# Gated linear attention: scores in four row groups, and the second direction prepared within the first

## The chip, the cores and the metric

The kernel runs on one core of one Trainium2 chip. The metric is the device time of one execution in microseconds (us), lower is better.

## The reference

Two layers of a trunk over 256 context rows and 512 latent rows (768 in all, width 1024). Each layer has four parallel branches (latent attention, mLSTM, gated linear attention, differential attention), merged by sigmoid gates and one projection, and then a mixture of 16 experts. The change is in the gated linear attention (GLA), which runs in both directions, first over the context, then over the latents. For 4 heads, 32 key and 64 value columns each, in chunks of 64 rows:

```
gcum = cumsum(lg)                       # log decay within the chunk
g_end = gcum[-1]
s_loc = (k * exp(g_end - gcum))^T v     # what a chunk adds to the state
S_next = exp(g_end) * S + s_loc         # carried from chunk to chunk
q_dec = q * exp(gcum)
att = causal( q_dec (k * exp(-gcum))^T )
o = att v + q_dec S                     # summed over the two directions
```

In layer 0 outputs are needed for all six tiles of 128 rows, in the last layer for the four latent tiles alone; the states run over all rows in both.

## The kernel before

**Engines and order.** Each engine has its own program, written out by hand, and semaphores tie them. The tensor engine (PE) does the projections with `fm` and `tm`, then `gla(L)`. The scalar engine (ACT) evicts projections and takes the exponentials, the vector engine (DVE) does sums, masks and evictions of the rest. The order of the `wait_ge` and `then_inc` calls in the three `gla(L)` functions is the order in which things happen; an engine never passes a waiting instruction of its own.

**Merge units.** `merge_units(L, n)` on PE does n units of the branches' merge: 8 products with a gate weight and 2 with a branch weight, into one PSUM bank. `gates` on ACT takes its tanh, `merged` on DVE multiplies and adds and then frees the bank (`g_free`). Layer 0 has 24 such units within GLA, layer 1 has 16; they come from the branch before, and so are work that PE can do at any time in GLA. `gl_quota` says how many are done at which place. `stir` is a filler: products whose result nobody reads.

**Banks.** `ring(kind, banks)` gives a kind of result its PSUM banks, used in turn; `job(kind)` waits until the next is free. In GLA the units ("g") have five banks (6, 7, 0, 1, 2), all else ("d") has 3, 4 and 5.

**Directions.** `for d in range(2)` is done whole, one direction after the other. For each: DVE makes the cumulated decays (a scan, L1808) and their differences, ACT takes the exponentials (L1597 is behind that wait), and DVE multiplies keys and queries, and copies the queries into `g_qm`, which holds zeros for all heads but one in each of its four blocks. PE transposes the decayed keys (L534), DVE copies them (`g_ke`). Then 11 state products on PE (L898, 64 rows each); DVE takes each out of its bank with a head mask and adds it to the decayed state in the row of states `g_S` (two operations). Then come a filler of 8 products, a wait for all states, and the tiles: the scores of a tile are one product of 128 rows and 512 columns (L908), DVE masks them (`g_A`), and the output is two products with the state (L919, 64 columns of the array each) and four with the values (L922), which DVE copies or adds into `g_y`.

**The end.** Two units (`GL_END`), a filler of 6 products, and the transposes of `g_y` once DVE has normed it. In `finish` DVE signals `y_ready` and only then merges the two units. The differential branch follows with its projections (L527).

The functions that the diff touches:

Of the kernel before, what the change touches and what calls it, by code (L numbers as in the profile page):

```python
# [22 lines left out]
P = 128  # L23
# [135 lines left out]
def hybrid_layers(nc, I, out, stop=None):  # L159
    ctx = ExitStack()  # L160
    with ctx:
# [31 lines left out]
        def pk(name):  # L193
# [13 lines left out]
                 "rows_in", "rows_t", "xs", "gu", "silu", "hid", "hid_t", "hid_f", "ys", "ys_a", "ys_d", "scat", "put", "sel_t", "sel_c", "fsum", "fsum_free", "df_ready"] + [f"f_back{t}" for t in range(NT)]  # L207
# [93 lines left out]
        def gl_quota(L):  # L301

            q = [(6, 2, (1, 0, 1, 0, 1, 1)), (4, 2, (1, 0, 1, 0, 1, 1))] if len(chunks(L)) == 3 else \
                [(5, 1, (1, 0, 1, 0)), (3, 1, (1, 0, 1, 0))]
            assert sum(a + b + sum(x) for a, b, x in q) + GL_END == branch_units(L)
            return q

# [74 lines left out]
        g_t1, g_t2 = area(4 * T, T), area(5 * T, T)  # L382
        g_a = area(6 * T, 2 * T).rearrange("p (d t) -> p d t", d=2)
        g_qd = area(6 * T, T)
        g_ki = area(7 * T, T)
        g_qm = area(8 * T, 4 * T).rearrange("p (h t) -> p h t", h=4)
        g_ke = area(12 * T, T)
        g_v = area(13 * T, NT * 256).rearrange("p (t c) -> p t c", t=NT)
        g_S = area(15 * T, 12 * 256).rearrange("p (c n) -> p c n", c=12)
        g_y = area(19 * T, NT * 256).rearrange("p (t c) -> p t c", t=NT)  # L390
        g_A = (area(21 * T, 512), g_t1[:, 0:512])
        g_sl = area(21 * T + 512, 256)
        g_sc = area(15 * T, NT * 256)

# [85 lines left out]
        def _(pe):  # L480
# [380 lines left out]
            def gla(L):  # L861
# [16 lines left out]
                quota = gl_quota(L)  # L878
# [6 lines left out]
                ring("g", (6, 7, 0, 1, 2))  # L885
                for d in range(2):

                    at_start, at_states, at_step = quota[d]
                    merge_units(L, at_start)
# [3 lines left out]
                    pe.wait_ge(sems["d_free"], st["d"])  # L893
                    for i in range(11):
# [3 lines left out]
                        pe.matmul(b[:, 0:256], g_ke[r:r + 64, t * P:(t + 1) * P], g_v[r:r + 64, t, :],  # L898
                                       start=True, stop=True).then_inc(sems["d_done"], 1)
                        if i == 5:  # L900
                            merge_units(L, at_states // 2)
# [4 lines left out]
                    def scores(t):  # L906
                        b = job("d")
                        pe.matmul(b[:, :].rearrange("p (h c) -> p h c", h=4), g_ki[:, t * P:(t + 1) * P],  # L908
                                       g_qm[:, :, t * P:(t + 1) * P], start=True, stop=True).then_inc(sems["d_done"], 1)

                    scores(QT[0])
                    for i, t in enumerate(QT):
                        if i + 1 < len(QT):
                            scores(QT[i + 1])
                        merge_units(L, at_step[i])
                        pe.wait_ge(sems["gl_att"], c.nth("gl_att"))
                        b = job("d")
                        for r in range(2):
                            pe.matmul(b[r * 64:r * 64 + 64, 0:256], g_qd[:, t * P + r * 64:t * P + r * 64 + 64],  # L919
                                      g_S[:, 2 * t + r, :], start=True, stop=False, skip_group_check=True)  # L920
                        for h in range(4):
                            ins = pe.matmul(b[:, h * 64:h * 64 + 64], g_A[i % 2][:, h * P:(h + 1) * P],  # L922
                                            g_v[:, t, h * 64:h * 64 + 64], start=False, stop=True, skip_group_check=True)
                        ins.then_inc(sems["d_done"], 1)
# [368 lines left out]
        def _(act):  # L1293
# [257 lines left out]
            def gla(L):  # L1551
# [29 lines left out]
                act.sem_inc(sems["gl_in"], 1)  # L1581
                for d in range(2):

                    do((g_t1, g_t2)[d], g_lg[:, d, :], AF.Abs)
                    do((g_t1, g_t2)[d], (g_t1, g_t2)[d], AF.Exp, scale=-1.0)
                    do((g_t1, g_t2)[d], (g_t1, g_t2)[d], AF.Ln, bias=ones[:, 0:1])
                act.sem_inc(sems["gl_l"], 1)
                quota = gl_quota(L)
                for d in range(2):
                    gates(L, 2 * (d == 0))  # L1590
                    act.wait_ge(sems["gl_g"], c.nth("gl_g"))

                    do(g_t1, g_t1, AF.Exp)
                    do(g_t2, g_lg[:, d, :], AF.Exp, scale=-1.0)
                    do(g_lg[:, d, :], g_lg[:, d, :], AF.Exp)
                    do(s_ge[:, d, :], s_ge[:, d, :], AF.Exp)
                    act.sem_inc(sems["gl_e"], 1)  # L1597
                    at_start, at_states, at_step = quota[d]
                    gates(L, at_start - 2 * (d == 0) + at_states + sum(at_step))
# [184 lines left out]
        def _(dve):  # L1784
# [387 lines left out]
            def gla(L):  # L2172
                quota = gl_quota(L)
                S(dve.memset(g_qm, 0.0))
                dve.wait_ge(sems["gl_in"], c.nth("gl_in"))
                dve.wait_ge(sems["gl_l"], c.nth("gl_l"))
                for d in range(2):
                    x = g_lg[:, d, :]
                    ts(x, x, 0.0, ALU.min)
                    tt(x, x, (g_t1, g_t2)[d], ALU.subtract)  # L2180
                    ts(x, x, 1.0 / 16, ALU.mult)
                merged(L, 2)
                for d in range(2):
                    x = g_lg[:, d, :]

                    xs_ = x if d == 0 else x[:, ::-1]
                    o_ = g_t2 if d == 0 else g_t2[:, ::-1]
                    scan(o_, cc("resets"), xs_, 0.0, ALU.mult, ALU.add)
                    copy(x, g_t2)
                    xc = x.rearrange("p (c l) -> p c l", l=64)  # L2190
                    end = xc[:, :, 63] if d == 0 else xc[:, :, 0]
                    copy(s_ge[:, d, :], end)
                    t1 = g_t1.rearrange("p (c l) -> p c l", l=64)
                    tt(t1, s_ge[:, d, :].unsqueeze(2).to_broadcast([P, 12, 64]), xc, ALU.subtract)
                    dve.sem_inc(sems["gl_g"], 1)
                    at_start, at_states, at_step = quota[d]
                    dve.wait_ge(sems["gl_e"], c.nth("gl_e"))
                    q0 = QS[-1][0]
                    tt(g_t1, g_t1, g_k, ALU.mult)
                    tt(g_ki, g_t2, g_k, ALU.mult)  # L2200
# [654 lines left out]
```

## Time and profile before

| | us |
|---|---|
| median of three runs | 3803.69 (3802.13 to 3811.6) |
| profiled execution, its own time | 3800.9 |
| its span | 3799.2 |
| PE busy | 3474.8 (91%) |
| DVE busy | 1117.7 (29%) |
| ACT busy | 716.6 (19%) |
| GLA of layer 0, from its first merge unit to the next branch | 581.7 to 764.5 |
| GLA of layer 1, likewise | 2548.3 to 2689.2 |

The span is what the profile sees; the execution's own time is 1.7 us more. Times of rows are counted from the span's start. A float32 product of two operands appears as two records on PE, a transpose as one. The granted clock of PE is 1.0 at 2.4 GHz and 0.5 at 1.2 GHz.

### The profile page before, as it was taken

To read this page: it belongs to the slowest core of one execution; us is meant where nothing else is said; L and a number is where in the kernel's file an instruction comes from. 1 tells how busy PE (TensorE), PEld (TensorE's weight loads), DVE (VectorE), ACT (ScalarE), POOL (GpSimd) and SP (SyncE) were. 2 spreads that over 40 slices of the span, in tenths; PEclk is the share of its full clock that TensorE was granted. 3 is DMA by queue.
4 is the path that set the end of the run, shared out by engine and by line. 5 is a ranking of instruction groups with operands and counts; after the bars stand their busy time and mean duration, and the time that the engine had idled before them with its cause. 6 is when DMAs were issued, how large, how long until landed. Compare 5 with 4: busy or idle time off the path is not lost.

```text
span 3799.2 us, 66279 instructions
## 1 busy us (share of the span) xinstructions
PE 3474.8 (91%) x27942; PEld 2414.8 (64%) x27942; DVE 1117.7 (29%) x2486; ACT 716.6 (19%) x1366; POOL 130.4 (3%) x188
## 2 busy tenths in 40 slices
PE   7899999999999999999999999998999998888887
PEld 4456756768875677766777666756677664444443
DVE  1433324425533411111111443315165231111112
ACT  2313212112223100000000422221132210010101
POOL 0000100000000000000000000000000000000000
PEclk9999999999999999999999999898999999999999
DMA  5511010020022999999999302020111259999998
GB/s 214 228 39 48 23 56 23 13 77 29 28 100 89 363 360 370 371 348 356 360 367 349 135 1 75 23 78 12 62 44 49 89 237 408 408 410 414 411 411 328
DMA packets 102941, 741.32 MB, mean 195 GB/s; under 512 B 8224, under 2 KB 14496, under 8 KB 60720
## 3 DMA queue, kind: packets, MB, share of 16 engines
q1 hardware_dynamic: 90512, 692.67, 46.3%
q0 software_dynamic: 12192, 45.14, 4.1%
q8 instruction: 191, 3.13, 0.3%
q14 instruction: 46, 0.38, 0.0%
HBM read 712.57 MB, written 25.21 MB: 194 GB/s over the span
## 4 chain that ended last, share of the span: by engine, by line
PE 67%; DMA 20%; DVE 6%; ACT 3%; issue 2%; SPq 0%; DVEq 0%; POOL 0%; ACTq 0%; POOLq 0%
PE psum L625 13%; PE psum L1127 10%; PE psum L527 7%; DMA ring<-in_w_e_down 7%; PE psum L520 5%; PE psum L1157 5%; DMA ring<-in_w_e_gate 4%; PE psum L983 4%; DMA work<-in_w_e_gate 3%; PE psum L627 3%; DMA ring<-in_w_e_up 3%; PE psum L1118 3%; DMA ring<-in_w_ada 2%; PE psum L852 2%; DVE work L1793 2%
## 5 line engine op out<-in xcount | busy, mean ns | idle before, releaser
L625 PE MATMUL psum<-HT,ring 128*128 128x256 f32 x2560 | 615.1, 396 | 19.3 <-DVEq L1871 8.5
L625 PEld LDWEIGHTS psum<-HT,ring 128*128 128x128 f32 x2560 | 502.0, 199 | 120.0 <-issue 29.6
L1127 PE MATMUL psum<-work,ring 128*64 128x96 f32 x11264 | 486.2, 247 | 49.3 <-issue 35.0
L1127 PEld LDWEIGHTS psum<-work,ring 128*64 128x64 f32 x11264 | 471.3, 137 | 66.1 <-issue 52.1
L1118 PE MATMUL psum<-ring,work 128*64 128x256 f32 x1024 | 253.1, 405 | 66.6 <-DMA ring<-in_w_e_gate 52.2
L1298 ACT ACTIVATE work<-psum,small 128x768 f32<-128x768 f32 (+3 forms) x208 | 146.0, 702 | 712.1 <-PE psum L1163 321.1
L527 PE MATMUL psum<-ring,HT 128*128 128x512 f32 (+1 forms) x768 | 276.0, 521 | 0.0
L1118 PEld LDWEIGHTS psum<-ring,work 128*64 128x64 f32 x1024 | 144.4, 145 | 162.9 <-DMA ring<-in_w_e_gate 62.8
L1119 PE MATMUL psum<-ring,work 128*64 128x256 f32 (+1 forms) x1024 | 244.0, 384 | 0.0
L1301 ACT ACTIVATE work<-psum 128x256 f32<-128x256 f32 (+8 forms) x227 | 107.4, 473 | 657.3 <-PE psum L527 236.9
L1157 PE MATMUL psum<-ring,work 128*64 128x512 f32 x960 | 220.1, 598 | 9.3 <-DMA ring<-in_w_e_down 9.3
L527 PEld LDWEIGHTS psum<-ring,HT 128*128 128x128 f32 x768 | 145.8, 190 | 127.3 <-issue 120.5
L520 PE MATMUL psum<-HT,ring 128*128 128x256 f32 (+5 forms) x688 | 216.1, 475 | 0.3 <-issue 0.3
L1797 DVE TENSOR_SCALAR work<-psum,small 128x64 f32<-128x64 f32 (+2 forms) x154 | 68.6, 445 | 457.6 <-PE psum L1163 204.4
L1298 ACT ACTIVATE X<-psum 128x384 f32<-128x384 f32 (+3 forms) x112 | 43.4, 387 | 732.9 <-PE psum L1127 411.0
L520 PEld LDWEIGHTS psum<-HT,ring 128*128 128x128 f32 (+2 forms) x688 | 123.2, 181 | 90.4 <-issue 76.0
L1298 ACT ACTIVATE YT<-psum,pack 128x256 f32<-128x256 f32 x160 | 75.9, 474 | 554.0 <-PE psum L627 503.6
L627 PE MATMUL psum<-YT 128*128 128x256 f32 x640 | 164.2, 379 | 0.0
L1793 DVE TENSOR_TENSOR work<-X,psum 128x384 f32<-128x384 f32 (+1 forms) x48 | 25.0, 521 | 416.8 <-PE psum L1127 416.8
L1157 PEld LDWEIGHTS psum<-ring,work 128*64 128x64 f32 x960 | 67.7, 136 | 123.0 <-issue 111.5
L983 PE MATMUL psum<-ring,X 128*128 128x512 f32 x320 | 140.5, 598 | 4.1 <-DVEq L2285 2.1
L1793 DVE TENSOR_TENSOR X<-X,psum 128x256 f32<-128x256 f32 (+1 forms) x64 | 22.5, 352 | 408.8 <-PE psum L1119 408.2
(208 smaller groups left out, 3981.3 us busy)
## 6 DMA issues: line engine op xcount, KB each, us to landing
ring<-in_w_e_gate SPq DMA_DIRECT2D x64, 2048.0 KB, 12.0
ring<-in_w_e_up SPq DMA_DIRECT2D x48, 2048.0 KB, 13.2
ring<-in_w_e_down SPq DMA_DIRECT2D x48, 2048.0 KB, 10.3
ring<-in_w_ada SPq DMA_DIRECT2D x24, 2048.0 KB, 9.9
ring<-in_w_e_up SPq DMA_DIRECT2D x32, 1536.0 KB, 10.8
ring<-in_w_gate SPq DMA_DIRECT2D x16, 2048.0 KB, 8.7
HT<-in_w_e_up SPq DMA_DIRECT2D x16, 2048.0 KB, 24.8
ring<-in_w_e_gate SPq DMA_DIRECT2D x16, 1536.0 KB
```

Source lines behind the costliest of these rows:

```text
L520: ins = pe.matmul(b[0:M, 0:n], w[:, k, c0:c0 + M], HT[:, k, off:off + n], start=(k == 0), stop=(k == KD - 1))
L527: ins = pe.matmul(b[:, 0:n], HT[:, k, t * P:(t + 1) * P], w[:, k, c0:c0 + n], start=(k == 0), stop=(k == KD - 1))
L625: pe.matmul(b[:, 0:256], w[:, k, d4 * P:(d4 + 1) * P], HT[:, k, off:off + 256], start=(k == 0), stop=(k == KD - 1))
L627: ins = pe.matmul(b[:, 256:512], wbr[:, m % 2, i, d4 * P:(d4 + 1) * P], YT[:, n_ % 2, i, off:off + 256], start=(i == 0), stop=(i == 1))
L983: ins = pe.matmul(b[:, :], mT[:, k, t * P:(t + 1) * P], w[:, k, :], start=(k == 0), stop=(k == KD - 1))
L1118: pe.matmul(b[0:64, 0:256], e_xs[:, k, 0:64], w[:, k, 0:256], start=(k == 0), stop=(k == KD - 1))
L1119: ins = pe.matmul(b[64:128, 0:n - 256], e_xs[:, k, 0:64], w[:, k, 256:n], start=(k == 0), stop=(k == KD - 1))
L1127: ins = pe.matmul(b[lo:lo + 64, f * cap:(f + 1) * cap], w[:, k, c0:c0 + 64], e_xs[:, k, 0:cap], start=(k == 0), stop=(k == KD - 1))
L1157: ins = pe.matmul(banks[6 + half][lo:lo + CAP_L, :], e_hidT[:, at, 0:CAP_L], w[:, k % 2 if split else k, half * 512:half * 512 + 512], sta ...
L1298: c.seq(act.activation(*a, **kw))
L1301: c.seq(act.activation(dst, src, AF.Copy))
L1793: S(dve.tensor_tensor(o_, a, b, op))
```

## The change

Scores: `g_qm` goes. Each tile's scores are now four products of 32 rows and 128 columns, one for each head, with keys and decayed queries as they lie in the partitions, each head into a bank of its own (0 to 3). Two tiles are done at a time, side by side in the four banks.

Order: the fillers of 8 products go. The first direction's 11 states are made in pieces of 4, 4 and 3 with a unit behind each, through four banks. The second direction's sums, exponentials, operands, transposed keys and states are made between the first direction's tiles, as `gl_ahead` says: for each tile whether keys are turned behind it, and which states come ahead of and behind its units. The states get a second row (`g_S[d]`). From the first scores on the units have two banks (6, 7) and all else has two (4, 5).

DVE's scaling by 1/16 moves into ACT's exponentials, and two of its operations become one. ACT takes the two logarithms' parts side by side and signals each.

```diff
+            q = (4, 3, ((2, 2, 1, 1, 1, 1), (2, 1, 1, 1, 1, 1))) if len(chunks(L)) == 3 else (4, 3, ((1, 1, 1, 1), (1, 1, 1, 0)))
...
+        def gl_ahead(L):
+            if len(qtiles(L)) == 6:
+                return (0, 0, 0, 0), (0, 0, 0, 0), (1, 0, 0, 0), (0, 0, 2, 4), (0, 4, 6, 8), (0, 8, 10, 11)
+            return (0, 0, 0, 0), (1, 0, 0, 0), (0, 0, 3, 6), (0, 6, 9, 11)
...
-                ring("g", (6, 7, 0, 1, 2))
-                for d in range(2):
...
-                    merge_units(L, at_states - at_states // 2)
-                    stir("g", 8)
...
+                ring("d", (2, 3, 4, 5))
+                ring("g", (6, 7, 0, 1))
+                merge_units(L, at_start)
+                opened = st["g"]
+                pe.wait_ge(sems["g_free"], opened - 2)
+                rings["g"].append((opened, (6, 7)))
...
+                def states(d, first, last):
+                    if last and not first:
+                        pe.wait_ge(sems["d_free"], st["d"])
+                    for i in range(first, last):
...
+                def scores(d, first):
+                    for i in range(first, first + 2):
+                        t = QT[i]
+                        at = (i % 2) * P
+                        for h in range(4):
+                            r = slice(32 * h, 32 * h + 32)
+                            ins = pe.matmul(g_scores[:, h, at:at + P], g_ki[d][r, t * P:(t + 1) * P], g_lg[r, d, t * P:(t + 1) * P],
+                                            start=True, stop=True)
+                    ins.then_inc(sems["gl_sc"], 1)
...
+                turn_keys()
+                for x in range(at_states):
+                    states(0, 4 * x, min(4 * x + 4, 11))
+                    merge_units(L, 1)
+                pe.wait_ge(sems["gl_ops"], c.nth("gl_ops"))
+                pe.wait_ge(sems["g_free"], opened)
+                ring("d", (4, 5))
+                scores(0, 0)
+                for d in range(2):
...
+                    for i in range(len(QT)):
+                        turn, a, b, z = gl_ahead(L)[i] if d == 0 else (0, 0, 0, 0)
+                        states(1, a, b)
+                        merge_units(L, at_step[d][i])
+                        states(1, b, z)
+                        if i % 2 == 0 and i + 2 < len(QT):
+                            pe.wait_ge(sems["gl_att"], gl_masked(L, d, i + 1))
+                            scores(d, i + 2)
+                        step(d, i)
+                        if turn:
+                            turn_keys()
```

ACT:

```diff
+                def decays(d):
+                    act.wait_ge(sems["gl_g"], c.nth("gl_g"))
+                    do(g_t1, g_t1, AF.Exp, scale=1.0 / 16)
                     act.sem_inc(sems["gl_e"], 1)
+                    do(g_lg[:, d, :], g_ki[d], AF.Exp, scale=1.0 / 16)
+                    do(g_ki[d], g_ki[d], AF.Exp, scale=-1.0 / 16)
+                    do(s_ge[:, d, :], s_ge[:, d, :], AF.Exp, scale=1.0 / 16)
+                    act.sem_inc(sems["gl_e"], 1)
...
+                gates(L, 2)
+                decays(0)
+                gates(L, at_start - 2 + at_states + at_step[0][0])
+                decays(1)
+                gates(L, sum(at_step[0][1:]) + sum(at_step[1]))
```

DVE, the tiles (`sums`, `keys` and `operands` are the parts of what was done ahead of each direction, `turned_keys` the copies of the transposed keys):

```diff
                     for i, t in enumerate(QT):
+                        turn, a, b, z = gl_ahead(L)[i] if d == 0 else (0, 0, 0, 0)
+                        states(1, a, b)
+                        merged(L, at_step[d][i])
+                        states(1, b, z)
                         dve.wait_ge(sems["d_done"], c.nth("d_done"))
...
+                        if i + 2 < len(QT):
+                            masked(d, i + 2)
+                        if d == 0:
+                            if i == 0:
+                                sums(1)
+                            if i == 1:
+                                keys()
+                                operands(1)
+                            if turn:
+                                turned_keys()
```

## Rows read from the trace of the kernel before

**Rows 1.** The page, the chain that ended last, by engine
```profile
PE 67%; DMA 20%; DVE 6%; ACT 3%; issue 2%; SPq 0%; DVEq 0%; POOL 0%; ACTq 0%; POOLq 0%
```
**Rows 2.** Windows of all engines: stretch, length, busy us (records) each, clock, DMA, GB/s
```profile
core 0: us, PE busy (x) PEld busy (x) DVE busy (x) ACT busy (x) POOL busy (x), PEclk, DMA share, GB/s
581.70:764.50 182.80, 168.89 (x761) 130.37 (x762) 86.96 (x163) 31.30 (x46) 0.00 (x0) 0.93 0.06 21
2548.30:2689.20 140.90, 129.69 (x540) 97.71 (x541) 70.71 (x136) 27.51 (x38) 0.00 (x0) 0.87 0.06 19
612.20:625.80 13.60, 9.86 (x23) 6.20 (x24) 9.60 (x23) 0.95 (x2) 0.00 (x0) 0.50 0.00 0
```
**Rows 3.** Timeline of PE, layer 0, first units and the first direction's states
```profile
start us, us, engine line op out<-in xcount [idle before <-releaser]
581.71 5.27 PE L625 MATMUL psum<-HT,ring 128*128 128x256 f32 x16 [1.09 <-ACTq L1580]
...
587.68 3.62 PE L625 MATMUL psum<-HT,ring 128*128 128x256 f32 x16
...
592.00 3.62 PE L625 MATMUL psum<-HT,ring 128*128 128x256 f32 x16
...
610.88 0.87 PE L534 MATMUL psum<-const,work 128*128 128x128 f32 x6 [1.45 <-DVEq L2204]
612.95 2.07 PE L898 MATMUL psum<-work 64*128 64x256 f32 x6 [1.19 <-DVEq L2209]
618.02 3.42 PE L898 MATMUL psum<-work 64*128 64x256 f32 x6 [2.99 <-DVEq L2219]
...
628.07 1.13 PE L898 MATMUL psum<-work 64*128 64x256 f32 x6
```
**Rows 4.** Timeline of PE, layer 0, filler, scores and output steps
```profile
635.56 3.62 PE L504 MATMUL psum<-const 128*128 128x256 f32 x16
639.01 1.88 PE L908 MATMUL psum<-work 128*128 128x512 f32 x4
640.73 3.62 PE L625 MATMUL psum<-HT,ring 128*128 128x256 f32 x16
...
645.14 0.65 PE L919 MATMUL psum<-work 128*64 128x256 f32 x4
...
646.66 1.08 PE L908 MATMUL psum<-work 128*128 128x512 f32 x2
```
**Rows 5.** Timeline of PE, differential branch, scores of 32 rows (two row groups)
```profile
854.71 0.70 PE L747 MATMUL psum<-work 32*128 32x256 f32 x4
855.34 0.33 PE L534 MATMUL psum<-const,work 128*128 128x128 f32 x1
```
**Rows 6.** Timeline of DVE, layer 0, the last row from layer 1
```profile
592.51 0.56 DVE L1797 TENSOR_SCALAR work<-work 128x768 f32<-128x768 f32 x1 [83.01 <-ACTq L1587]
...
598.92 1.76 DVE L1808 TENSOR_TENSOR_SCAN work<-const,work 128x768 f32<-128x768 f32 x1
...
618.58 0.42 DVE L1793 TENSOR_TENSOR work<-psum,const 128x256 f32<-128x256 f32 x1
...
619.68 0.42 DVE L1793 TENSOR_TENSOR work<-psum,const 128x256 f32<-128x256 f32 x1
...
640.14 0.69 DVE L1793 TENSOR_TENSOR work<-psum,const 128x512 f32<-128x512 f32 x1 [2.85 <-PE psum L908]
...
645.80 0.42 DVE L1805 SCALAR_TENSOR_TENSOR YT<-YT,psum 128x256 f32<-128x256 f32 x1 [4.03 <-ACTq L1351]
...
761.29 0.42 DVE L1805 SCALAR_TENSOR_TENSOR YT<-YT,psum 128x256 f32<-128x256 f32 x1
...
2687.29 0.42 DVE L1805 SCALAR_TENSOR_TENSOR YT<-YT,psum 128x256 f32<-128x256 f32 x1
```
**Rows 7.** Timeline of ACT, layer 0, the exponentials of one direction
```profile
602.56 2.59 ACT L1298 ACTIVATE work<-work 128x768 f32<-128x768 f32 x3 [7.66 <-DVEq L2195]
```
**Rows 8.** Timeline of PE, units after the last step (749.55, 2677.05), layer 1's second
```profile
749.55 3.67 PE L625 MATMUL psum<-HT,ring 128*128 128x256 f32 x16
...
2555.70 3.62 PE L625 MATMUL psum<-HT,ring 128*128 128x256 f32 x16
...
2677.05 3.67 PE L625 MATMUL psum<-HT,ring 128*128 128x256 f32 x16
```

More of the change, by code:

```diff
@@ L911, in gla @@
[L911 to L924, printed above, removed]
+                                  start=True, stop=True).then_inc(sems["d_done"], 1)
@@ new lines, in step @@
+                def step(d, i):
+                    t = QT[i]
+                    pe.wait_ge(sems["gl_att"], gl_masked(L, d, i))
+                    b = job("d")
+                    for r in range(2):
+                        pe.matmul(b[r * 64:r * 64 + 64, 0:256], g_lg[:, d, t * P + r * 64:t * P + r * 64 + 64],
+                                  g_S[d][:, 2 * t + r, :], start=True, stop=False, skip_group_check=True)
+                    for h in range(4):
+                        ins = pe.matmul(b[:, h * 64:h * 64 + 64], g_A[i % 2][:, h * P:(h + 1) * P],
+                                        g_v[:, t, h * 64:h * 64 + 64], start=False, stop=True, skip_group_check=True)
+                    ins.then_inc(sems["d_done"], 1)
@@ L2172, in gla @@
             def gla(L):
[L2173 to L2177, printed above, removed]
-                    x = g_lg[:, d, :]
[L2179 to L2194, printed above, removed]
+                at_start, at_states, at_step = gl_quota(L)
@@ L2195, in gla, with keys @@
                     dve.sem_inc(sems["gl_g"], 1)
[L2196 removed]
+                def keys():
                     dve.wait_ge(sems["gl_e"], c.nth("gl_e"))
[L2198 removed]
                     tt(g_t1, g_t1, g_k, ALU.mult)
[L2200 to L2203 removed]
@@ L2209, in gla, with states @@
                         dve.sem_inc(sems["d_free"], 1)
-                    merged(L, at_start - 2 * (d == 0))
-                    heads = cc("heads").unsqueeze(2).to_broadcast([P, 4, 64])
-                    S(dve.memset(g_S[:, gla_chunk(d, 0), :], 0.0))
-                    for i in range(11):
+                def states(d, first, last):
+                    if last and not first:
+                        S(dve.memset(g_S[d][:, gla_chunk(d, 0), :], 0.0))
+                    for i in range(first, last):
                         a, z = gla_chunk(d, i), gla_chunk(d, i + 1)
@@ L2234, in gla, with masked @@
-                    masked(0)
+                        stt(g_S[d][:, z, :], g_S[d][:, a, :], s_ge[:, d, a:a + 1], g_sl, ALU.mult, ALU.add)
+                    if last == 11 and first < last:
+                        dve.sem_inc(sems["gl_state"], 1)
+                def masked(d, i):
+                    mask = cc(("m_fwd", "m_bwd")[d]).unsqueeze(1).to_broadcast([P, 4, P])
+                    at = (i % 2) * P
+                    if i % 2 == 0:
+                        dve.wait_ge(sems["gl_sc"], c.nth("gl_sc"))
+                    tt(g_A[i % 2].rearrange("p (h c) -> p h c", h=4), g_scores[:, :, at:at + P], mask, ALU.mult)
+                    dve.sem_inc(sems["gl_att"], 1)
@@ new lines, in gla @@
+                dve.wait_ge(sems["gl_in"], c.nth("gl_in"))
+                sums(0)
+                merged(L, 2)
+                keys()
+                operands(0)
+                merged(L, 1)
+                turned_keys()
+                merged(L, at_start - 3)
+                for x in range(at_states):
+                    states(0, 4 * x, min(4 * x + 4, 11))
+                    if x:
+                        merged(L, 1)
+                masked(0, 0)
+                masked(0, 1)
+                merged(L, 1)
```

97 lines of the change are left out of this document (44 added, 53 removed).

## The prediction

> **What bounds the kernel now.** The page comes first: the chain that ended last runs 67% through the tensor engine and 20% through DMA [rows 1], and its DMA parts are weights of the experts and of the modulation, not of this branch. The change touches two stretches, the gated linear attention of layer 0 (182.8 us) and of layer 1 (140.9 us) [rows 2]. In both the tensor engine (PE) is the engine to follow: the projections before it and the differential branch after it start when PE gets to them, so what a stretch loses or gains moves the end one for one. The timeline shows where PE doesn't do dense work there: it waits for the first operands (1.45 us), for the copied keys (1.19) and for VectorE (DVE), which evicts the states (2.99) [rows 3]. Around these waits the granted clock is half (0.50, which is 1.2 GHz) for 13.6 us [rows 2]; of PE's 9.9 busy us there about half, 4.9, is the clock's price. Then come 16 filler records, 635.56 to 639.01, 3.45 us, and the scores of two tiles take 1.72 us [rows 4].
>
> **Prices.** A merge unit (20 records) is 4.32 us of PE (587.68 to 592.00); the first one of a stretch is slow, 5.97 us in layer 0, 7.4 in layer 1 [rows 3, 8]. One output step (both halves of the carried state, four heads) is 1.52 us, 645.14 to 646.66 [rows 4]. Six records (three state products) take 1.13 us, part of it latency [rows 3]: I take 0.25 us a product. DVE: a state costs 1.10 us (618.58 to 619.68), the scan 1.76, masking a tile 0.69, an operation on 256 columns 0.42, so a merge of two 1.0 with its gaps; it begins about 0.75 us after PE's last product of the unit, for ScalarE's tanh lies between [rows 4, 6]. ScalarE (ACT) needs for three exponentials 2.59 us [rows 7].
>
> **What is removed.** (1) Two fillers of 3.45 us a layer: 13.8 us in all. (2) The states' lumps. Before, PE sits behind the state chain of 11 x 1.1 us in both directions, with at most one or two units as cover. Now the first direction's eleven are cut by three units, the second's lie between units of the first's steps. Waits of 1.45, 1.19 and 2.99 us and the half clock behind them go, but see the new waits. DVE's early work (scaling, a copy, the masked queries) goes as well. It waits till 592.51 for both directions' logarithms [rows 6]; with one it starts some 3 us earlier, at 589 by my estimate, and sums (4.0), exponential, two merges (2.1) and a multiplication (1.0) make the first keys by 597, while PE asks for them at 600.6. The first wait is gone, and DVE's removed operations themselves count for nothing, since PE's units cover them (uncovered they would be 7 us a direction). (3) The scores. Per tile there were 512 columns in one product; now four products of 32 rows and 128 columns, each in its own bank.
>
> **Price of the scores.** No row shows four groups at once. Two groups of 32 rows do stand there: four records of 256 columns from 854.71 to 855.34, 0.63 us [rows 5], where four such records of full height take 0.86 (a fifth of a unit's 20 records). So groups overlap; 0.43 us is what one group streams, 0.2 is load and drain. Two tiles on four groups stream 0.43 us as well: with the same 0.2 and some issue time I take 0.75 a pair of tiles. The bounds are 0.65 and, without overlap, today's 1.72. Ten pairs (6 in layer 0, 4 in layer 1) save 9.7 us by it, 0 at the other bound. The Trainium skill (TensorEngine Tiling (Array Packing), Theoretical Speedup) allows up to 4x for 32 rows; that would be 0.43 a pair, 3 us more gained and a time of 3755. The same page (Key Properties) says that a change of tiling mode drains the engine, which speaks against cutting products small: each pair now has two such changes. The trace agrees: ahead of the step's 64-column tiles a unit takes 4.41 us instead of 4.32 [rows 3, 4], 0.1 us, which is inside my 0.2.
>
> **The new waits, layer 0.** From 581.7: 22 units up to the last step (5.97 + 21 x 4.32 = 96.7), 6 score pairs 4.5, 12 steps 18.2, 22 states 5.5, keys turned twice 1.4: 126.3 us of PE. Waits: the first keys' copies 1.35 (as 612.95 shows). Where the second direction's keys are turned, behind step 2 of the first, PE needs the bank of that step's output, and DVE copies the output, masks a tile (0.69) and then the keys (1.26): 2.2 us. The ring for states and outputs has now two banks. In tiles 3 and 4 two states follow a unit at once, and the output step then needs the bank of the first of them, which DVE reads only behind tanh and merge: 0.75 + 1.0 + 0.45 after the unit's end, less 0.45 of PE's own work: 1.8 us, twice; twice 0.5 for the state that waits for the output's copy; 0.4 for the last state. Together 8.6 us. The last step ends at 581.7 + 134.9 = 716.6, before at 749.55 [rows 8]: 33.0 us earlier. For the clock behind these waits of 1.8 to 2.2 us I charge 2.5 us (a half-clock spell costs 1.65 us as at 581.71 to 4.9 as at 612.2; some of them will meet one).
>
> **Layer 1.** 14 units 7.4 + 13 x 4.32 = 63.6, scores 3.0, 8 steps 12.2, states 5.5, keys 1.4: 85.7 us. Here the keys are to be turned after step 1 already, and only one unit and one step (5.8 us) lie between step 0 and that. What must happen behind step 0 is a chain over two queues: output copied 0.7, tile masked 0.85, DVE's sums for direction 1 (subtraction 0.96, scan 1.76, ends 0.2, difference 0.96: 4.0), ACT's exponentials 2.9. Behind these in ACT's queue stands the tanh of unit 9 (0.6), behind that in DVE's queue its merge 1.1, the copy 0.45, masking 0.75, and then the keys' multiplication 1.0, with 0.3 of handovers: 12.6 us. **PE stands 6.8 us**, then 2.3 more while DVE finishes queries and copies keys. The tiles 2 and 3 take three states each after and before their unit on two banks: 2.6, 0.9 and 1.85 us by the reckoning above, and 1.35 at the start: 15.8 us of waits, and 4.5 for the clock (one full spell, a part of another). The last step ends at 2548.3 + 106.0 = 2654.3, before at 2677.05, where the unit behind it starts [rows 8]: 22.7 us earlier, the clock counted.
>
> **The tail.** The filler at the end (12 records of 0.216 us, 2.6) stays, but the merge units now go through two banks where there were five. It must therefore wait for the merge of the last unit but one, and that stands in DVE's queue behind the whole head norm: at 761.29, 11.7 us after the last step, in layer 1 at 2687.29, 10.2 us after it [rows 6, 8]. Two units cover 8.7 us of that. In layer 0 PE idles 3.6 us, then fills 2.6, then turns the outputs over two banks: 17.2 us from the last step to the next branch where there were 14.9. In layer 1 14.3 where there were 12.2. With a clock spell behind 3.6 us of idling (3.4 us, between the 1.65 and 4.9 above) and a third of one in layer 1: 5.7 and 3.1 us given back.
>
> **Sum.** Layer 0: 33.0 - 2.5 - 5.7 = 24.8. Layer 1: 22.7 - 3.1 = 19.6. Together 44.4 us. The profiled execution took 3800.9 us (span 3799.2), 2.8 below the median of 3803.7: 3756.5 by the one, 3759.3 by the other; I take 3758. Nothing later should eat it: what DMA has in the chain lies elsewhere [rows 1], and loads are issued when a buffer is freed, so they move along with PE.
>
> **Rivals.** *The row groups don't overlap* (that part of the change does nothing). For it: no row shows more than two at once. Against: those two do [rows 5]. 9.7 us less: 3768.
> *The clock falls behind each new wait.* There are eight places of 1.8 us or more; at 4.9 us each that is 39 us, where I charged 11.4: 3786. For it: 1.45 and 1.19 us close together were enough at 612.2 [rows 2, 3]. Against: most new waits stand alone between dense units.
> *Slower than before:* the first direction's steps run at half clock throughout, since a wait returns every 6 us there. Its 11 units in layer 0 and 7 in layer 1 would cost 4.32 us more each, 78, of which 7 are charged: 3829. It decides from 13 of these 18 units on. Against: with waits up to 3 us in their lumps, the stretches of before still keep a mean clock of 0.93 and 0.87 [rows 2].
> *The gain is given back* in the expert stages, where DMA has its 20% of the chain: 3800. For it: they don't get shorter. Against: they begin with loads asked for only when this branch and the next are through.
>
> **How the numbers follow.** Forecast 0.67, no overlap 0.12, clock at each wait 0.13, given back 0.05, slower 0.03. The likeliest's own range is 3745 to 3772: at one end the clock holds (11 us less) and scores take 0.65 (1 less), at the other its price is half as high again (6) and layer 1's queues lag by some 8 us more. The range 3744 to 3778 takes in the first rival and leaves out the last two, most of the second and a little of the first, some 0.2. A measurement of this kernel can tell about 0.3% (11 us) from no change. Faster by more: 0.67 + 0.12 + 0.13 = 0.92; within: 0.05; slower: 0.03.
>
> **What would show it.** In the changed profile: no 16-record filler in the stretches; score groups of 32 rows, 16 records within 0.75 us (1.7 would be the first rival); in layer 1 an idle time of about 6.8 us before keys are transposed, released by DVE, and none such in layer 0; idle times near 1.8 us before steps that follow states; before the last filler 3.6 us in layer 0 and 2.0 in layer 1, released by DVE's merge; stretches of about 158 and 121 us. The prediction is wrong if the stall in layer 1 is absent (9 to 12 us more gained), if a stretch's granted clock falls below 0.85, or if the time between and behind the stretches changes.

## The result, and the profile after

The changed kernel takes **3778.07 us** (median of 6, 3772.09 to 3788.13), the kernel before 3806.78 on the same chip (6, 3802.13 to 3811.6): ratio **0.993, 95% interval 0.9915 to 0.9945**. It is faster, by 28.7 us, where 3758 was forecast (a gain of 45.7 from 3803.69). The range ended at 3778, and 3778.07 lies just above it.

The page's chain that ended last reads nearly as before [rows 1]:

```profile
PE 69%; DMA 21%; DVE 5%; ACT 2%; issue 2%; SPq 0%; DVEq 0%; POOL 0%; ACTq 0%; POOLq 0%
```

The two stretches, from the first unit to the differential branch, and a part of layer 0, as windows; they answer to [rows 2]:

```profile
580.40:748.50 168.10, 157.22 (x801) 125.16 (x801) 79.69 (x150) 28.76 (x44) 0.00 (x0) 0.91 0.08 28
2535.90:2665.60 129.70, 113.66 (x556) 89.09 (x557) 64.27 (x123) 24.96 (x36) 0.00 (x0) 0.87 0.10 32
650.90:681.60 30.70, 27.17 (x96) 19.52 (x97) 12.63 (x29) 0.95 (x2) 0.00 (x0) 0.72 0.00 1
```

They are 14.7 and 11.2 us shorter than before, 25.9 together. The granted clock is no better: 0.91 and 0.87, where it was 0.93 and 0.87. In the third row it is 0.72.

PE's timeline of the changed kernel, layer 0: first unit, states and scores (answering to [rows 3, 4]), the steps that carry the second direction's states, and the tail [rows 8]; then layer 1.

```profile
580.41 6.47 PE L633 MATMUL psum<-HT,ring 128*128 128x256 f32 x16 [1.09 <-ACTq L1620]
...
587.59 3.62 PE L633 MATMUL psum<-HT,ring 128*128 128x256 f32 x16
...
596.22 3.62 PE L633 MATMUL psum<-HT,ring 128*128 128x256 f32 x16
...
600.54 0.82 PE L542 MATMUL psum<-const,work 128*128 128x128 f32 x6
602.63 1.13 PE L914 MATMUL psum<-work 64*128 64x256 f32 x8 [1.27 <-DVEq L2254]
...
608.20 1.14 PE L914 MATMUL psum<-work 64*128 64x256 f32 x8
609.27 3.72 PE L633 MATMUL psum<-HT,ring 128*128 128x256 f32 x16
...
613.78 1.13 PE L914 MATMUL psum<-work 64*128 64x256 f32 x6
...
619.35 0.73 PE L924 MATMUL psum<-work 32*128 32x128 f32 x16
620.01 3.72 PE L633 MATMUL psum<-HT,ring 128*128 128x256 f32 x16
...
651.03 1.23 PE L914 MATMUL psum<-work 64*128 64x256 f32 x4 [1.81 <-DVEq L2254]
652.19 4.74 PE L633 MATMUL psum<-HT,ring 128*128 128x256 f32 x16
...
660.13 0.65 PE L934 MATMUL psum<-work 128*64 128x256 f32 x4 [1.70 <-DVEq L2265]
...
664.13 5.58 PE L633 MATMUL psum<-HT,ring 128*128 128x256 f32 x16
...
672.91 0.65 PE L934 MATMUL psum<-work 128*64 128x256 f32 x4 [1.70 <-DVEq L2265]
...
676.39 6.27 PE L633 MATMUL psum<-HT,ring 128*128 128x256 f32 x16
...
728.02 3.67 PE L633 MATMUL psum<-HT,ring 128*128 128x256 f32 x16
...
740.30 5.49 PE L512 MATMUL psum<-const 128*128 128x256 f32 x12 [3.42 <-DVEq L1918]
...
2595.25 1.54 PE L542 MATMUL psum<-const,work 128*128 128x128 f32 x6 [6.74 <-DVEq L2239]
2598.49 1.23 PE L914 MATMUL psum<-work 64*128 64x256 f32 x4 [1.70 <-DVEq L2254]
2600.36 1.22 PE L914 MATMUL psum<-work 64*128 64x256 f32 x2 [0.64 <-DVEq L2265]
2601.51 6.28 PE L633 MATMUL psum<-HT,ring 128*128 128x256 f32 x16
...
2649.60 3.67 PE L633 MATMUL psum<-HT,ring 128*128 128x256 f32 x16
...
2660.37 4.54 PE L512 MATMUL psum<-const 128*128 128x256 f32 x12 [1.92 <-DVEq L1918]
```

The reader is to see three things. The waits stand where they were forecast and nearly as long: 1.27, 1.81, twice 1.70, 6.74, then 3.42 and 1.92 ahead of the last filler. Two tiles' scores take 0.66 us (619.35 to 620.01), so the four row groups do overlap. And the 16 records of a unit, 3.62 us at full clock, take 4.74, 5.58 and 6.27 behind waits of 1.7 to 1.8 us, and 6.28 in layer 1: that is the clock, whose mean over this part is 0.72 (third window).

### The profile page after: what moved, and what is told of

Its sections match the earlier page's. It is cut to its first block, busy times and chain, and to the rows that moved or that the text cites. A ratio compares the mean times of both kernels' runs of the same rounds, so it can differ in the third digit from the quotient of the medians.

```text
span 3778.2 us, 66347 instructions
## 1 busy us (share of the span) xinstructions
PE 3457.1 (92%) x27998; PEld 2409.6 (64%) x27998; DVE 1099.1 (29%) x2456; ACT 711.7 (19%) x1362; POOL 130.8 (3%) x188
## 4 chain that ended last, share of the span: by engine, by line
PE 69%; DMA 21%; DVE 5%; ACT 2%; issue 2%; SPq 0%; DVEq 0%; POOL 0%; ACTq 0%; POOLq 0%
PE psum L633 14%; PE psum L1167 8%; PE psum L535 7%; DMA ring<-in_w_e_down 7%; PE psum L1197 6%; PE psum L528 5%; DMA ring<-in_w_e_gate 5%; DMA ring<-in_w_e_up 4%; PE psum L1023 4%; PE psum L635 3%; PE psum L1158 3%; PE psum L755 2%; DMA work<-in_w_e_gate 2%; PE psum L1203 2%; PE psum L773 2%
## 5 line engine op out<-in xcount | busy, mean ns | idle before, releaser
L1197 PEld LDWEIGHTS psum<-ring,work 128*64 128x64 f32 x960 | 68.8, 137 | 123.8 <-issue 113.7
## 6 DMA issues: line engine op xcount, KB each, us to landing
HT<-in_w_e_up SPq DMA_DIRECT2D x16, 2048.0 KB, 24.8
```

The source lines that it names most:

```text
L1197: ins = pe.matmul(banks[6 + half][lo:lo + CAP_L, :], e_hidT[:, at, 0:CAP_L], w[:, k % 2 if split else k, half * 512:half * 512 + 512], sta ...
```

## The experiments

Each kernel was run beside the kernel before, both on the same chip; the ratio is to that kernel, and kernels of different chips are compared by it. The table takes the two stretches of each profile together, from windows like those above. **Idle** is length less PE's busy time. **Clock** is (1 - granted clock) x length for each stretch, added: what the lower clock costs if PE is busy throughout, so an upper bound, and good to some 1.5 us, since the clock is given to 0.01.

| kernel | ratio (95%) | stretches | sum | idle | clock |
|---|---|---|---|---|---|
| before | 1 | 182.8, 140.9 | 323.7 | 25.1 | 31.1 |
| b_nofill | 0.9956 (0.9938-0.9975) | 175.1, 134.5 | 309.6 | 26.1 | 31.1 |
| changed | 0.993 (0.9915-0.9945) | 168.1, 129.7 | 297.8 | 26.9 | 32.0 |
| a_again | 0.9933 (0.9912-0.9953) | 168.2, 129.3 | 297.5 | 26.9 | 31.9 |
| e_serial | 0.995 (0.9934-0.9967) | 165.5, 127.7 | 293.2 | 26.9 | 26.9 |
| e_fill | 0.9882 (0.9854-0.991) | 157.8, 119.8 | 277.6 | 3.0 | 5.6 |
| e_beside | 0.9979 (0.9965-0.9992) | 166.2, 135.1 | 301.3 | 26.5 | 11.4 |
| e_thin32 | 0.9928 (0.99-0.9956) | 161.5, 130.3 | 291.8 | 1.9 | 20.8 |
| e_thin64 | 0.9893 (0.9863-0.9923) | 157.8, 118.5 | 276.3 | 2.7 | 4.4 |
| e_sums_early | 0.9917 (0.9891-0.9943) | 166.2, 119.2 | 285.4 | 21.5 | 21.1 |
| e_states_first | 0.9898 (0.9874-0.9921) | 164.9, 122.0 | 286.9 | 25.5 | 21.3 |
| e_tail | 0.9923 (0.9892-0.9953) | 159.9, 125.9 | 285.8 | 22.7 | 23.1 |
| e_best1 | 0.9889 (0.9873-0.9906) | 160.3, 113.6 | 273.9 | 15.3 | 16.0 |
| e_best2 | 0.9917 (0.99-0.9933) | 160.3, 112.6 | 272.9 | 9.8 | 14.8 |
| e_fill_sums | 0.987 (0.9851-0.9888) | 158.9, 113.2 | 272.1 | 3.3 | 6.6 |
| e_best3 | 0.985 (0.983-0.987) | 156.5, 108.6 | 265.1 | 4.0 | 4.2 |

**The changed kernel again** (a_again, unaltered).

> The changed kernel unaltered, as the measure for the two beside it. 3778 us, ratio to before 0.993; stretches about 168 and 130 us with half-clock spells behind the new waits.

The stretches repeat within 0.4 us. The rest doesn't repeat: between the stretches this execution took 1774.4 us (743.0 to 2517.4) where the first took 1787.4 (748.5 to 2535.9), in one and the same code. So the stretches are read to a microsecond from one profile, and the total only from its interval. Even a stretch can move: e_serial's layer 0, with the same 10.9 us of waits, is 2.6 us shorter at a clock of 0.93.

**Fillers in the new waits** (e_fill): if the waits take the clock, products whose result nobody reads give it back.

```diff
                 turn_keys()
+                stir("g", 3)
...
+                        if b and not a:
+                            stir("g", 4)
                         states(1, a, b)
                         merge_units(L, at_step[d][i])
                         states(1, b, z)
+                        if d == 0 and z - b == 2:
+                            stir("g", 4)
...
                         if turn:
+                            if L == 1:
+                                stir("g", 15)
                             turn_keys()
                 merge_units(L, GL_END)
+                stir_bank(banks[0], 8 if L == 0 else 4)
                 stir("g", 6)
```

Four more stand before layer 1's third state of tile 2.

> The changed kernel with filler products put into its new waits on PE, about as long as each wait (1.3 us for the first copied keys, 1.7 before each output step behind states and for the second copied keys, 6.5 in layer 1 before the keys are turned, 3.5 and 1.7 before the last filler); the waits themselves stay. If the half clock behind the waits is what the forecast had too small, the slow units, products and fillers behind them (11 us in each layer by the profile after) come back: some 22 us less than the changed kernel, about 3756 us, and a mean clock of 0.98 or more in both stretches. If the slow stretches have another cause (products of 64 rows, transposes), the time stays within 5 us of the changed kernel's 3778.

Windows of e_fill, both stretches, and layer 0 around the states:

```profile
576.30:734.10 157.80, 156.71 (x847) 126.01 (x848) 79.72 (x150) 28.75 (x44) 0.00 (x0) 0.98 0.09 29
2515.20:2635.00 119.80, 117.86 (x625) 94.27 (x626) 64.33 (x123) 24.95 (x36) 0.00 (x0) 0.98 0.09 30
643.50:674.00 30.50, 30.17 (x151) 21.93 (x150) 16.22 (x36) 1.42 (x3) 0.00 (x0) 1.00 0.10 32
```

And the filler in layer 1's long wait, from its timeline:

```profile
2567.32 6.69 PE L512 MATMUL psum<-const 128*128 128x256 f32 x30
```

The clock is 1.00 where it was 0.72. 57 products of 0.432 us, 24.6 us, took the place of 23.9 us of idle time (26.9 less 3.0), and still the stretches are 20.2 us shorter: 20.2 + 24.6 - 23.9 = **20.9 us is the clock's price** behind the new waits, by this balance.

**Is it the idle time, or what stands around it?** The same 57 fillers, behind the waits instead of in them (e_beside), and the fillers in the waits but over 32 or 64 rows (e_thin32, e_thin64). In e_beside they stand behind the states, the output step or the old filler that waited. The 15 of the long wait come later: behind it are first the turned keys, a further wait and three states, then these fillers, from 2606.75 on.

```diff
                         states(1, a, b)
+                        if b and not a:
+                            stir("g", 4 if L == 0 else 19)
                         merge_units(L, at_step[d][i])
...
                         step(d, i)
+                        if d == 0 and z - b == 2:
+                            stir("g", 4)
```

> The same 57 filler products as in the run with fillers in the waits, but each put behind the instruction that waited, so that the waits stay. They are 24.6 us of products (57 x 0.432). If the waits themselves lower the clock, nothing is won back: idle time 27 and clock cost about 29 us as in the changed kernel, stretches about 178 and 144 us, time 3803, ratio to before 1.000. If it was the thin work around the waits (products of 32 and 64 rows) and full products close by repair it, the clock cost falls to the 5.5 us of the first units: stretches about 167 and 134 us, time 3781, ratio 0.994.

PE's timeline of e_beside, layer 0 and the long wait of layer 1, and its two windows:

```profile
654.85 0.70 PE L914 MATMUL psum<-work 64*128 64x256 f32 x4 [1.81 <-DVEq L2263]
655.48 2.00 PE L512 MATMUL psum<-const 128*128 128x256 f32 x8
657.32 3.62 PE L633 MATMUL psum<-HT,ring 128*128 128x256 f32 x16
...
664.13 0.65 PE L936 MATMUL psum<-work 128*64 128x256 f32 x4 [1.70 <-DVEq L2274]
...
2600.49 1.54 PE L542 MATMUL psum<-const,work 128*128 128x128 f32 x6 [6.73 <-DVEq L2248]
...
2606.75 9.68 PE L512 MATMUL psum<-const 128*128 128x256 f32 x38
```
```profile
582.90:749.10 166.20, 155.31 (x847) 125.76 (x848) 79.65 (x150) 28.73 (x44) 0.00 (x0) 0.98 0.08 29
2541.30:2676.40 135.10, 119.53 (x625) 95.64 (x626) 64.24 (x123) 24.93 (x36) 0.00 (x0) 0.94 0.09 31
```

The waits are all there (26.5 us idle), and in layer 0 none lowers the clock, not the one of 3.4 us at the tail either. In layer 1 it still falls at the wait of 6.73 us (the six records behind it take 1.54 us, 0.82 at full clock). So my theory, that each wait takes the clock, falls: with full products close behind, the waits of 1.6 to 1.8 us cost themselves alone in this profile. The stretches are as the second theory had them, 166 and 135 for 167 and 134. The time, 3789.93, is 9 us above its forecast, and the ratio 0.005 (19 us) above the changed kernel's, of which the stretches explain 3.5 us; the rest lies outside them and isn't explained.

```diff
+                    pe.matmul(b[:, 0:256], ident[0:32, :], const[0:32, 0:256], start=True, stop=True)
```

> The fillers stand in the waits as in the run that filled them, same number and same 256 columns each, but every product is over 32 rows of the array instead of 128 (only the 6 products of the old filler at the end keep 128). PE is then busy in the waits all the same. If idle time is what takes the clock, it holds as with full fillers: granted clock 0.98 in both stretches, 158 and 120 us, ratio to before 0.988. If rows count, so that thin products are as good as none, the clock falls where it fell in the changed kernel: granted clock about 0.91 and 0.87, stretches about 168 and 130 us, ratio 0.993.

> The same with fillers over 64 rows, the height of the state products. If idle time takes the clock: 0.98, stretches 158 and 120 us, ratio 0.988. If rows count: between that and the changed kernel, granted clock about 0.95 and 0.92, stretches about 163 and 125 us, ratio 0.990.

PE's timeline of e_thin32, the tail of layer 0, then layer 1:

```profile
735.48 4.26 PE L516 MATMUL psum<-const 32*128 32x256 f32 x16
739.67 5.49 PE L512 MATMUL psum<-const 128*128 128x256 f32 x12
...
2587.47 8.81 PE L516 MATMUL psum<-const 32*128 32x256 f32 x30
2596.22 1.54 PE L552 MATMUL psum<-const,work 128*128 128x128 f32 x6
```

PE is not idle there (0.9 us in the whole stretch of layer 1), and the clock falls all the same: 30 records take 8.81 us where the 30 of full height in e_fill take 6.69, and layer 1's mean is 0.89. The 64-row ones hold it as the full ones do (0.98, 0.99). In layer 0's middle even the 32-row ones, 8 records at a time, hold it; only its tail falls, where 16 of them take 4.19 us (735.48 to 739.67), and the 12 full-height records behind them 5.49. What these runs show is that the clock fell behind idle time and behind long busy time of 32 rows alike, and that short waits with dense work close behind did not bring it down. The Trainium skill (TensorE: Matmul & The Clock Gate, HAM oscillation) explains the loss by idle gaps; e_thin32 shows a loss without a gap.

**The waits one by one.** Layer 1's long wait: the second direction's sums before the first masks, and its keys behind tile 0 instead of 1 (e_sums_early). DVE takes the states ahead of the merge (e_states_first). No wait before the last filler (e_tail).

```diff
+                sums(1)
                 masked(0, 0)
                 masked(0, 1)
...
                             if i == 0:
-                                sums(1)
-                            if i == 1:
                                 keys()
                                 operands(1)
```
```diff
                         states(1, a, b)
-                        merged(L, at_step[d][i])
                         states(1, b, z)
+                        merged(L, at_step[d][i])
```
```diff
                 merge_units(L, GL_END)
-                stir("g", 6)
+                stir_bank(banks[0], 6)
+                ring("d", (3, 4, 5))
```

In the first, ACT's exponentials move ahead of the steps' gates too.

> The changed kernel, with the second direction's sums on DVE ahead of the first masks and its exponentials on ACT ahead of the unit's tanh that follows, and its keys and queries one tile earlier. If layer 1's wait of 6.74 us is the chain of sums, exponentials, tanh and merge, 1 to 3 us of it are left and the spell behind it is shorter: 5 to 9 us less, 3769 to 3773 us. If DVE's queue as a whole is the limit there, the wait only moves to the first scores and the time stays.

> The changed kernel, only DVE takes the states behind a unit before it merges that unit. If the output step waits for a bank because the merge stands ahead of the state in DVE's queue, the waits of 1.70 us (two in layer 0) and 1.60, 0.49 and 1.69 (layer 1) shrink to 0.7 or less, 5 to 6 us, and with them go the half-clock spells of layer 0's last two tiles and part of layer 1's: 10 to 17 us less than the changed kernel, 3761 to 3768 us. If the two banks themselves are too few, whatever the order, the waits stay and so does the time (3778).

> The changed kernel with the last filler in bank 0, which is free, so that it doesn't wait for the merge of the last unit but one, and three banks for the transposes behind it. If that wait (3.42 and 1.92 us) and the half clock behind it are the tail's loss, the time from the last step to the next branch goes from 20.5 to 15 us in layer 0 and from 16.0 to 12.2 in layer 1: 9 us less, 3769 us. If the tail is bound by the head norm (signalled 11.6 us after the last step) it gains 5 us or less.

PE's timeline of e_sums_early, layer 1; then of e_states_first, layer 0:

```profile
2588.24 1.10 PE L937 MATMUL psum<-work 128*128 128x64 f32 x8
2589.18 0.61 PE L542 MATMUL psum<-const,work 128*128 128x128 f32 x4
```
```profile
665.51 0.65 PE L934 MATMUL psum<-work 128*64 128x256 f32 x4 [0.73 <-DVEq L2265]
...
668.63 0.70 PE L914 MATMUL psum<-work 64*128 64x256 f32 x2 [0.80 <-DVEq L2309]
669.25 3.72 PE L633 MATMUL psum<-HT,ring 128*128 128x256 f32 x16
...
678.32 1.22 PE L914 MATMUL psum<-work 64*128 64x256 f32 x2 [0.80 <-DVEq L2309]
679.47 6.24 PE L633 MATMUL psum<-HT,ring 128*128 128x256 f32 x16
```

The 6.74 us are gone, as their cause, DVE's and ACT's queues, would have it; layer 1 is 10.5 us shorter. In e_states_first each 1.70 became 0.73 or 0.74 and a new 0.80: the sum of idle time is hardly smaller (25.5), yet the stretches are 3.2 and 7.7 us shorter, for the clock's bound went from 32.0 to 21.3. The first such pair of waits left the clock up (the unit behind it takes 3.72), the second brought it down (6.24).

One wait and its neighbours don't settle it, then. The wait of 1.81 us ahead of the second direction's first states, with the same products around it, was followed by a slow unit in the changed kernel (4.74) and by one at full clock in e_sums_early, whose layer 0 differs only in DVE's and ACT's order:

```profile
652.71 0.70 PE L914 MATMUL psum<-work 64*128 64x256 f32 x4 [1.81 <-DVEq L2254]
653.35 3.72 PE L633 MATMUL psum<-HT,ring 128*128 128x256 f32 x16
```

So the single spells can't be booked to single waits; the sums over a stretch can be compared. e_tail takes 8.2 and 3.8 us from the stretches, the idle time and the slow filler; by its total alone it can't be told from the changed kernel.

**The parts of the gain.** The four heads' scores issued head by head (e_serial), and the kernel before without its four fillers (b_nofill: `stir("g", 8)` left out).

```diff
-                    for i in range(first, first + 2):
...
-                        for h in range(4):
+                    for h in range(4):
+                        for i in range(first, first + 2):
```

> The changed kernel with the score products of a pair of tiles issued head by head, so that neighbours in the queue share a row group and can't overlap. If the overlap of the four groups is what makes a pair take 0.66 us, it goes to 1.5 to 1.8 us, and ten pairs cost 8 to 11 us more than in the changed kernel: 3787. If order doesn't matter to the overlap, the pair stays at 0.7 and the time at 3778.

> The kernel before without its four fillers of 16 records (3.45 us each), nothing else. If they cover no wait and keep no clock, all of it is gained: 13.8 us less than before. If they hide the end of the state chain or hold up the clock, 5 us or less.

```profile
618.81 0.75 PE L924 MATMUL psum<-work 32*128 32x128 f32 x16
619.49 3.72 PE L633 MATMUL psum<-HT,ring 128*128 128x256 f32 x16
```

Head by head the 16 records of e_serial take 0.68 us (above), tile by tile they took 0.66. So the order of issue within the group is of next to no account. b_nofill gains 7.7 and 6.4 us of its stretches, 14.1 where 13.8 were booked, and costs no clock (31.1 before and after): half of what the change takes off its stretches is to be had by this alone.

**Together.** e_best1 is the three edits of the waits. e_best2 adds 3 and 4 fillers where the keys are copied, e_best3 also 2 in each wait of 0.7 us or more among the states. e_fill_sums is e_fill with the early sums and without the 15.

> The changed kernel with three edits at once: states ahead of the merge on DVE, the second direction's sums early, the last filler in a free bank. Their stretches alone were 3.2, 1.9 and 8.2 us shorter in layer 0 and 7.8, 10.5 and 3.8 in layer 1 than the changed kernel's 168.1 and 129.7. If each takes away its own wait and the spell behind it, they add up: 155 and 110 us (the edits of layer 1 share some spells), 30 to 35 us less than the changed kernel, some 3745. If they only shift one limit of DVE's queue, the sum is nearer to the best single one: 3765.

> As the one with three edits, and fillers of 1.3 us while the first keys are copied and of 1.7 us while the second direction's are. If the two spells left come from these waits, a clock of 1.0 from there on, 2 to 5 us less than without the fillers; if the waits alone are too short to lower the clock, no change.

> The fillers in the waits (all but the one of 15 products in layer 1), and the second direction's sums and keys made earlier, so that the 6.8 us wait of layer 1 which that filler covered is gone. If clock and wait are two separate costs, both gains add: stretches 158 and about 111 us, 28 us less than the changed kernel, 3748, ratio to before 0.986. If the filler in the long wait was hiding the same cost as the early sums remove, it stays at the 0.988 of the fillers alone.

> States ahead of the merge, early sums, no wait at the tail, and fillers of 2 to 4 products in every wait of 0.7 us or more that was left. If even waits of 0.73 and 0.80 us cost the clock, it is now 1.0 throughout both stretches: 152 and 108 us, about 3745, ratio to before 0.985. If those short waits did not lower the clock, no gain over the same kernel without fillers (3757, ratio 0.989).

PE's timeline of e_best2, and windows of e_best3 behind the slow first unit:

```profile
653.67 0.65 PE L934 MATMUL psum<-work 128*64 128x256 f32 x4 [0.73 <-DVEq L2269]
...
656.78 1.22 PE L914 MATMUL psum<-work 64*128 64x256 f32 x2 [0.80 <-DVEq L2314]
657.93 6.23 PE L633 MATMUL psum<-HT,ring 128*128 128x256 f32 x16
```
```profile
587.00:737.70 150.70, 147.77 (x818) 118.12 (x817) 79.12 (x149) 23.10 (x39) 0.00 (x0) 1.00 0.06 19
2530.00:2631.20 101.20, 100.11 (x557) 79.19 (x556) 63.75 (x122) 17.87 (x29) 0.00 (x0) 1.00 0.06 17
```

e_best1 fell between its two forecasts: its three edits had taken 35.3 us from the stretches one by one, together they take 23.9, so they share spells or waits. In e_best2 two waits of 0.73 and 0.80 us among 64-row states still bring half the clock. Its time came out 7 us above e_best1's, with stretches 1.0 us shorter. With 0.9 us of products in each of them (e_best3) the clock is 1.00 to the end, the stretches 7.8 us shorter, the time **3743.87 us (3740.15 to 3755.93), ratio 0.985**: the best kernel, 29 us ahead of the changed one beside it (3772.91); its layer 0 is 4.5 us longer than forecast. e_fill_sums had stretches of 158.9 and 113.2 us for 158 and 111: wait and clock are two costs, and both gains add, but for some 3 us.

## Why the prediction was right, and where wrong

**Right by mechanism.** PE sets the stretches. The long wait of layer 1 measured 6.74 us for 6.8; the waits that follow states 1.70 for 1.8, and the tail's 3.42 and 1.92 for 3.6 and 2.0, in the places named. Up to the last step the waits sum to 6.7 us (8.6) and 14.1 (15.8). The first keys' wait was taken as 1.35, though its row has 1.19 [rows 3]; it measured 1.27. Scores are 0.66 a pair for 0.75, so the rival without overlap is out. The fillers were worth 14.1 us for 13.8.

**The term that failed: the clock.** By its own sum the prediction had stretches of 158.0 and 121.3 us (182.8 - 24.8, 140.9 - 19.6); they are 168.1 and 129.7, 18.5 us longer. It said "2.5 us" for layer 0's waits, 4.5 for layer 1, and 3.4 and 1.0 for the tails, 11.4 together. e_fill's balance gives 20.9, so some 9.5 us more.

The places say which of these four failed. From the last step on, the tails took 20.5 us for 20.6 and 16.0 for 15.3. Up to the last step the stretches took 147.6 us for 137.4 and 113.7 for 106.0, 17.9 of the 18.5 us. Counted from the rows of the changed kernel, each slow group against the same group at full clock (as the units at 652.19, 664.13 and 676.39, 5.5, 6.4 and 7.1 us to the next instruction, against 4.51), the clock cost about 9 us in layer 0 and 10 in layer 1 up to the last step, and 3 and 2 in the tails. So the 2.5 and 4.5 us are what was mis-sized, and the tails' 4.4 us held. This count, some 23 to 24 us in all, is an estimate as the balance is.

The reason that stood against the second rival, "most new waits stand alone between dense units", is what failed, and e_beside shows how: they don't stand alone. Products of 64 rows stand before or behind each, and the next wait comes 9 to 13 us later (651.03, 660.13, 672.91); where full products stand close behind the same waits, the clock holds. Which of the two, the thin products or the nearness of the next wait, weighs more isn't shown. That rival, at 4.9 us for each of eight waits, 39 us, was too dear: the measured price lies between the two. The table says it most shortly. Idle time went from 25.1 to 26.9 us and the clock's bound from 31.1 to 32.0: the change took nothing off either. Its 25.9 us are work taken out, the fillers (14.1 in b_nofill) and the scores (10 pairs by 1.72 - 0.66, 10.6, read from rows; no run puts the old scores back), and little more. The prediction had booked a lower cost of the clock besides.

**A second, smaller term: the changes of tile.** A unit between units is 4.32 us (596.22 to 600.54), one between 64-row products 4.51 (609.27 to 613.78). Such handovers stand around some 15 groups of units in layer 0 and 10 in layer 1, now that states, scores and steps are cut small: 0.1 to 0.19 us each, 2.5 to 4.7 us. The prediction saw 0.1 us and put it into the scores alone. A state is 0.27 us only among four (608.20 to 609.27), where 0.25 was taken; two alone take 0.63 (654.85 to 655.48 in e_beside), and the 44 states of both layers and directions, in groups of one to four, some 14.4 us at full clock for 11.0. And layer 0's first unit is 7.18 us for 5.97, 1.2 more, layer 1's 7.36 (2535.88 to 2543.24) for 7.4. With the clock by e_fill's balance, these and the shorter waits (3.6 us in favour) account for some 14 of the 18.5 us, with the clock counted by rows for some 17.

**Given back elsewhere:** between the stretches 1787.4 us against 1783.8, behind them 1112.6 against 1110.0 (each span less its stretches' ends). a_again, the same code, has 1774.4 and 1113.4: no effect of the change can be read there. Over all sixteen profiles the part between runs from 1774.4 to 1800.2 us. In the profiled execution what lies outside the stretches came out 4.9 us longer than before (1.3 us less ahead of the first stretch is taken off); with the 18.5 us in them this makes its 3779.97 us, for which 3756.5 was forecast.

**What stays open.** How much of the lowered clock comes by the height of the products and how much by idle time isn't settled as a rule, only for these arrangements: 30 and 16 records of 32 rows lost it, 8 did not in layer 0's middle, and one and the same wait lowered it in one kernel and not in another. And e_best1 and e_best2, with nearly equal stretches, differ by more in their totals than the profiles of the two explain.

## What to carry to other kernels

When work is cut into small pieces to fill a wait, sum idle time and the clock's cost over the whole stretch before and after: here both stayed, and only what was no longer computed was gained. A wait of one or two microseconds between short products of few rows was often charged twice here, once as itself and once in the dense work behind it; a filler of its length or a little less, in place of it or right behind it, paid where the clock would fall, and the first choice is to reorder the releasing engine's queue so that the wait goes. Look at the spread of a second profile of the same kernel before reading anything into a part that the change doesn't touch.

## What the runs showed of the hardware that was not expected

- Half clock came after waits of only 0.73 and 0.80 us among states of 64 rows (e_best2, a unit's 16 records 6.23 us instead of 3.72), though not after each such pair (e_states_first, 3.72 behind the first), and not after waits of 1.81, 1.70 and 3.41 us with eight or more full-height records close behind (e_beside, 0.98 in layer 0).
- It came without idle time too: within 30 records of 32 rows that kept PE busy (8.81 us for 6.69 at full height, e_thin32). With 64 rows it did not (e_thin64, 0.98 and 0.99).
- Four row groups of 128 columns: 16 records in 0.66 us, where two tiles by full-height products took 1.72 [rows 4], 2.6 times less; 0.68 when issued head by head. The Trainium skill (TensorE: Matmul & The Clock Gate, Measured speedup vs the span model) has 3.07 times for four row groups of 512 columns; no run here shows that length.
